# A routing chain rewritten with scans and one slot table, and TensorE products that nobody reads

## What is computed

```
h2 = x * (1 + sc2) + sh2
gl = h2 @ grp_w + grp_b                 # 4 groups
g_idx, pg_top = argmax(gl), softmax(gl)[g_idx]
sel = (h2 @ exp_w + exp_b).reshape(T, 4, 8)[g_idx]
vals, idx = top_k(sel, 2)               # 2 of the 8 experts of that group
w = pg_top * softmax(vals)
y += w_e * ((silu(h2 @ w_gate[e]) * (h2 @ w_up[e])) @ w_down[e])   # for the chosen e
```

## Time and profile before

| | |
|---|---|
| median of 3 runs | 1684.97 us (1683.86 to 1691.19) |
| profiled execution | 1687.71 us |
| its span, first to last instruction | 1684.5 us |
| mean granted TensorE clock | 0.938 of full |
| PE busy | 1506.4 us (89%) |
| DVE busy | 942.9 us (56%) |

### The profile page before, as it was taken

The page is one execution under the profiler, slowest core; times in us unless marked ns, Lnnn a source line. Parts: engine busy times, 40 slices in busy tenths (PEclk is TensorE's granted clock), DMA queues, the critical chain, the costliest instruction groups (busy, mean ns, idle before and its releaser), DMA issues. The chain is left out here.

```text
span 1684.5 us, 22742 instructions
## 1 busy us (share of the span) xinstructions
PE 1506.4 (89%) x8546; PEld 1091.8 (65%) x8546; DVE 942.9 (56%) x1580; ACT 370.5 (22%) x710; POOL 368.4 (22%) x624
## 2 busy tenths in 40 slices
PE   6689988999996999849999988998299999999985
PEld 2467766444444788638888874554288888888852
DVE  3867875466635999975665641534623333333326
ACT  2553342011110111135755550100000000000004
POOL 0330230111110000000312237654122122122204
PEclk9799999999998999979999988999579999999998
DMA  9422113233330221130000013113249898898845
GB/s 290 169 68 82 60 57 131 89 112 108 118 116 19 82 69 57 50 110 1 2 1 2 2 48 128 63 63 123 77 171 327 325 332 333 324 337 322 302 175 222
DMA packets 102965, 230.28 MB, mean 137 GB/s; under 512 B 12807, under 2 KB 70727, under 8 KB 94120
## 3 DMA queue, kind: packets, MB, share of 16 engines
q1 hardware_dynamic: 78968, 195.86, 32.8%
q0 software_dynamic: 10960, 20.80, 3.5%
q10 hardware_dynamic: 12960, 12.59, 2.2%
HBM read 204.66 MB, written 40.01 MB: 145 GB/s over the span
## 5 line engine op out<-in xcount | busy, mean ns | idle before, releaser
L1086 PE MATMUL PS<-buffer 128*128 128x128 f32 (+8 forms) x5674 | 1263.9, 381 | 107.5 <-DVE buffer L1576 52.0
L1086 PEld LDWEIGHTS PS<-buffer 128*128 128x128 f32 (+2 forms) x5674 | 879.7, 196 | 464.0 <-issue 309.0
L1576 DVE TENSOR_TENSOR buffer<-buffer 128x256 f32<-128x256 f32 (+18 forms) x467 | 264.8, 587 | 20.2 <-ACT buffer L836 5.6
L1089 PE MATMUL PS<-buffer 128*128 128x128 f32 x1176 | 166.7, 285 | 34.0 <-DVE buffer L1576 24.6
L1089 PEld LDWEIGHTS PS<-buffer 128*128 128x128 f32 x1176 | 137.9, 156 | 63.2 <-issue 49.1
L1576 DVE TENSOR_TENSOR buffer<-PS,buffer 128x512 f32<-128x512 f32 (+3 forms) x143 | 94.0, 684 | 144.2 <-PE PS L1086 126.2
L1576 DVE TENSOR_TENSOR buffer<-buffer,PS 128x256 f32<-128x256 f32 (+3 forms) x55 | 27.5, 501 | 206.4 <-PE PS L1086 195.8
L1996 DVE TENSOR_SCALAR_CACHE_REDUCE buffer<-PS 128x1152 f32<-128x1152 f32 (+1 forms) x72 | 89.2, 1239 | 41.5 <-PE PS L1086 40.5
L979 ACT ACTIVATE buffer<-buffer 128x1152 f32<-128x1152 f32 (+1 forms) x72 | 83.7, 1163 | 103.8 <-DVE buffer L1996 103.8
L1060 ACT ACTIVATE buffer<-PS 128x256 f32<-128x256 f32 x33 | 12.7, 384 | 371.3 <-PE PS L1086 293.3
L2012 DVE COPY buffer<-PS 128x640 f32<-128x640 f32 x64 | 52.8, 825 | 60.5 <-PE PS L1089 60.5
(11 more groups left out here) (162 smaller groups left out, 930.5 us busy)
## 6 DMA issues: line engine op xcount, KB each, us to landing
buffer<-in_exp_w_gate SPq DMA_DIRECT2D x33, 1024.0 KB
buffer<-in_exp_w_up SPq DMA_DIRECT2D x33, 1024.0 KB
buffer<-in_exp_w_down SPq DMA_DIRECT2D x33, 1024.0 KB
buffer<-in_w_mod SPq DMA_DIRECT2D x24, 1024.0 KB, 7.6
filter_spectra<-buffer ACTq DMA_DIRECT2D x88, 128.0 KB, 1.7
buffer<-filter_spectra SPq DMA_DIRECT2D x44, 256.0 KB, 2.6
buffer<-in_w_in SPq DMA_DIRECT2D x9, 1024.0 KB, 5.5
buffer<-expert_outputs SPq DMA_DIRECT2D x4, 1536.0 KB, 17.1
```

Of the source, the lines that this page charges most:

```text
L1086: return nc.tensor.matmul(out, lhsT, rhs, start=start, stop=stop)
L1089: return nc.tensor.transpose(out, in_, ident)
L1576: return dve.tensor_tensor(out, a, b, op)
```

## The change

1. Ahead of the routing chain: for the last tile DVE takes the logits of tile 6 before the moments rather than after `h2`; it makes `h2` from `resid` directly with two fused instructions, and `xnorm` behind it. POOL's last `x1` waits for `xnorm` (`xnorm_ready`).
2. Instructions that depend on no token move from the chain to a place before the first norm, with new tables (`overflow_base`, `tile_starts`, the token numbers in `slot_value`). The matrix `upper` becomes upper minus all-ones, since the table of running sums now includes the own tile.
3. The chain: the softmax exponents are shifted later and used later; the sum over tiles is one scan (`tensor_tensor_scan`) over data laid out expert by expert; the blocks come from a scaled and rounded count, their running sum from a scan; the block list is made last. Token number and weight lie side by side (`slot_value`), so one table `r_pair` 100 wide takes the place of `r_number` and `r_tok`, in two halves, one for each choice.
4. PE: 18 products for slots rather than 36, 9 of them after the first half; and `keep_clock`: 6, 8 and 4 products 256 columns wide of the identity with the tables, into bank 7, which nobody reads.
5. POOL gathers block 0 with `slot_token` as its index, without the copy.

The diff, cut where lines only move or rename:

```diff
@@ -213,7 +213,8 @@
-        mix_w = keep.take(2 * NTILE, "p (c t) -> p c t", c=2)
+        slot_value = keep.take(4 * NTILE, "p (c t s) -> p c t s", c=2, t=NTILE)
+        mix_w = slot_value[:, :, :, 1]
...
@@ -222,6 +223,8 @@
+        overflow_base = decay[:, 304:304 + NEXP]
+        tile_starts = mod_ring.rearrange("p r n -> p (r n)")[:, 0:NTILE * NEXP]
...
@@ -327,20 +330,21 @@
-        r_all = rt.take(NTILE * NEXP, "p (t n) -> p t n", t=NTILE)
-        r_before = rt.take((NTILE + 1) * NEXP, "p (t n) -> p t n", t=NTILE + 1)
-        r_count = rt.take(NEXP)
+        r_all = rt.take(NTILE * NEXP)
+        r_upto = rt.take(NTILE * NEXP)
...
-        r_scan = rt.take(2 * NEXP, "p (r n) -> p r n", r=2)
+        r_ends = rt.take(NEXP)
...
+        r_pair = rt.take(4 * NTILE * MAX_BLOCKS, "p (i s n) -> p i s n", i=2 * NTILE, s=2)
...
@@ -708,7 +712,7 @@
-                    pool.wait_ge(sem("h2_ready"), NTILE)
+                    pool.wait_ge(sem("xnorm_ready"), NTILE)
...
@@ -751,7 +755,10 @@
-            gather_rows(1, slice(0, 1), 1)
+            pool.indirect_dma_start(
+                out=xg[:, 1, :], out_offset=None, in_=h2_d[:, :],
+                in_offset=bass.IndirectOffsetOnAxis(ap=slot_token[:, 0:1], axis=0),
+                bounds_check=last_token, oob_is_err=False).then_inc(sem("xg_loaded1"), 16)
...
@@ -1477,28 +1484,31 @@
+            def keep_clock(count):
+
+                for i in range(count):
+                    mm(bank(7, 2 * P), ident, tables[:, 0:2 * P])
+
+            keep_clock(6)
...
-            flat = "p t n -> p (t n)"
-            mm(bank(0, NTILE * NEXP), upper, r_all[:, :, :].rearrange(flat), True, False)
-            mm(bank(0, NTILE * NEXP), ones, r_before[:, 0:NTILE, :].rearrange(flat), False, True)
-            mm(bank(1, NEXP), ones, r_before[:, NTILE, :]).then_inc(sem("routing_product"), 1)
+            mm(bank(0, NTILE * NEXP), upper, r_all, True, False)
+            mm(bank(0, NTILE * NEXP), ones, r_upto, False, True)
+            mm(bank(1, NEXP), ones, r_upto.rearrange("p (n t) -> p n t", t=NTILE)[:, :, NTILE - 1]).then_inc(sem("routing_product"), 1)
...
-            pe.wait_ge(sem("routing_ready"), 2)
-            for i in range(2 * NTILE):
-                last = mm(bank(4, MAX_BLOCKS), r_hot[:, i, :], r_number[:, i, :], i == 0, i == 2 * NTILE - 1)
+            keep_clock(8)
+            for c in range(2):
+                pe.wait_ge(sem("routing_ready"), 2 + c)
+                for i in range(NTILE * c, NTILE * (c + 1)):
+                    last = mm(bank(4, 2 * MAX_BLOCKS), r_hot[:, i, :], r_pair[:, i, :, :].rearrange("p s n -> p (s n)"),
+                              i == 0, i == 2 * NTILE - 1)
...
-            pe.wait_ge(sem("route_done"), 1)
+            pe.wait_ge(sem("control_ready"), 1)
...
+            keep_clock(4)
...
@@ -2035,26 +2045,42 @@
+                if t == NLAT:
+                    take_logits(t - 2)
...
-                give(dve.tensor_scalar(xnorm, resid, bn[:, 12:13], bn[:, 14:15], ALU.subtract, ALU.mult), "xnorm_ready")
...
-                    own(tt(h2, xnorm, sc2[1], ALU.mult))
-                    tt(h2, h2, sh2[1], ALU.add).then_inc(sem("h2_ready"), 1)
+                    own(dve.scalar_tensor_tensor(h2, resid, bn[:, 12:13], sc2[1], ALU.subtract, ALU.mult))
+                    dve.scalar_tensor_tensor(h2, h2, bn[:, 14:15], sh2[1], ALU.mult, ALU.add).then_inc(sem("h2_ready"), 1)
...
+                give(dve.tensor_scalar(xnorm, resid, bn[:, 12:13], bn[:, 14:15], ALU.subtract, ALU.mult), "xnorm_ready")
...
+            own(dve.tensor_scalar(overflow_base, first_slot, -1.0, float(P * (NEXP - 1)), ALU.mult, ALU.add))
...
+            own(dve.tensor_copy(slot_value[:, :, :, 0], token_no[:, 0:2 * NTILE].rearrange("p (c t) -> p c t", c=2)))
+            sub(upper, upper, ones)
+            for r in range(2):
+                dve.wait_ge(sem(f"mod_stored{r}"), 16 * ((MOD_CHUNKS - COND_CHUNKS) // 2))
+            own(dve.memset(tile_starts, 1.0))
+            own(dve.memset(tile_starts.rearrange("p (n t) -> p n t", t=NTILE)[:, :, 0], 0.0))
...
-                if t >= 3:
+                if t >= 3 and t != NTILE:
...
@@ -2073,101 +2099,80 @@
-            give(tt(r_g, groups, r_max.unsqueeze(2).broadcast_to([P, NTILE, NGRP]), ALU.subtract), "exponents_shifted")
-            dve.wait_ge(sem("exponents_taken"), 1)
-            own(dve.tensor_reduce(r_pg, r_exp, AX.X, ALU.add))
-            own(dve.reciprocal(r_pg, r_pg))
...
+            four = [P, NTILE, NGRP, EPG]
...
-            give(tt(r_d, r_v[:, 1, :], r_v[:, 0, :], ALU.subtract), "exponents_shifted")
-            dve.wait_ge(sem("exponents_taken"), 2)
...
-            own(tt(r_all, r_mask[:, 0, :, :], r_mask[:, 1, :, :], ALU.add))
-            own(dve.memset(r_before[:, 0, :], 0.0))
-            for t in range(NTILE):
-                ins = tt(r_before[:, t + 1, :], r_before[:, t, :], r_all[:, t, :], ALU.add)
-                own(ins) if t + 1 < NTILE else give(ins, "routing_ready")
...
+            own(tt(r_all.rearrange("p (n t) -> p t n", t=NTILE), r_mask[:, 0, :, :], r_mask[:, 1, :, :], ALU.add))
+            give(dve.tensor_tensor_scan(r_upto, tile_starts, r_all, 0.0, ALU.mult, ALU.add), "routing_ready")
+
+            give(tt(r_exp, groups, r_max.unsqueeze(2).broadcast_to([P, NTILE, NGRP]), ALU.subtract), "exponents_shifted")
+            give(tt(r_d, r_v[:, 1, :], r_v[:, 0, :], ALU.subtract), "exponents_shifted")
+
...
-            own(dve.tensor_copy(r_count, bank(1, NEXP)))
-            own(dve.tensor_scalar(r_blocks, r_count, float(P), None, ALU.is_gt))
-            for m in range(2, NTILE):
-                own(dve.scalar_tensor_tensor(r_blocks, r_count, float(P * m), r_blocks, ALU.is_gt, ALU.add))
...
+            count = bank(1, NEXP)
+            own(dve.tensor_scalar(r_blocks, count, 1.0 / P, -(0.5 + 0.5 / P), ALU.mult, ALU.add))
+            own(dve.tensor_scalar(r_blocks, r_blocks, ROUND_MAGIC, None, ALU.add))
+            own(dve.tensor_scalar(r_blocks, r_blocks, -ROUND_MAGIC, 0.0, ALU.add, ALU.max))
+            own(dve.tensor_tensor_scan(r_ends, ones[:, 0:NEXP], r_blocks, 0.0, ALU.mult, ALU.add))
+            sub(r_base, r_ends, r_blocks)
+            axpy(r_base, r_base, float(P), overflow_base)
+            rank = bank(0, NTILE * NEXP).rearrange("p (n t) -> p t n", t=NTILE)
...
-            for c in range(2):
-                own(tt(r_mask[:, c, :, :], r_mask[:, c, :, :], r_slot, ALU.mult))
-                own(dve.tensor_reduce(r_pos[:, NTILE * c:NTILE * (c + 1)], r_mask[:, c, :, :], AX.X, ALU.add))
+            own(tt(r_slots, r_mask, r_slot.unsqueeze(1).broadcast_to([P, 2, NTILE, NEXP]), ALU.mult))
+            own(dve.tensor_reduce(r_pos, r_slots.rearrange("p c t n -> p (c t) n"), AX.X, ALU.add))
...
-            give(tt(r_number, r_tok, token_no[:, 0:n].unsqueeze(2).broadcast_to(blocks_last), ALU.mult), "routing_ready")
-            give(tt(r_tok, r_tok, mix_w.rearrange("p c t -> p (c t)").unsqueeze(2).broadcast_to(blocks_last), ALU.mult), "routing_ready")
+            dve.wait_ge(sem("exponents_taken"), 2)
+            own(dve.tensor_reduce(r_pg, r_exp, AX.X, ALU.add))
+            own(dve.reciprocal(r_pg, r_pg))
+            own(dve.tensor_scalar(r_max, r_d, 1.0, None, ALU.add))
+            own(dve.reciprocal(r_max, r_max))
+            own(tt(mix_w[:, 0, :], r_pg, r_max, ALU.mult))
+            own(tt(mix_w[:, 1, :], mix_w[:, 0, :], r_d, ALU.mult))
+            for c in range(2):
+                i0, i1 = NTILE * c, NTILE * (c + 1)
+                own(tt(r_hot[:, i0:i1, :], row128.unsqueeze(1).broadcast_to([P, NTILE, P]),
+                       r_rowblk[:, 0, i0:i1].unsqueeze(2).broadcast_to([P, NTILE, P]), ALU.is_equal))
+                own(tt(r_blk[:, i0:i1, :], row128[:, 0:MAX_BLOCKS].unsqueeze(1).broadcast_to([P, NTILE, MAX_BLOCKS]),
+                       r_rowblk[:, 1, i0:i1].unsqueeze(2).broadcast_to([P, NTILE, MAX_BLOCKS]), ALU.is_equal))
+                both = [P, NTILE, 2, MAX_BLOCKS]
+                give(tt(r_pair[:, i0:i1, :, :], r_blk[:, i0:i1, :].unsqueeze(2).broadcast_to(both),
+                        slot_value[:, c, :, :].unsqueeze(3).broadcast_to(both), ALU.mult), "routing_ready")
+
+            blocks_first = [P, MORE_BLOCKS, NEXP]
+            own(tt(r_cmp, r_ends.unsqueeze(1).broadcast_to(blocks_first),
+                   row128[:, 0:MORE_BLOCKS].unsqueeze(2).broadcast_to(blocks_first), ALU.is_le))
+            own(dve.tensor_reduce(r_eid[:, 0:MORE_BLOCKS], r_cmp, AX.X, ALU.add))
+            own(dve.tensor_scalar(control[:, NEXP:MAX_BLOCKS], r_eid[0:1, 0:MORE_BLOCKS], float(NEXP - 1), None, ALU.min))
+            own(dve.tensor_scalar(control[:, 61:62], r_ends[0:1, NEXP - 1:NEXP], float(NEXP), None, ALU.add))
+            give(dve.tensor_scalar(control[:, 60:61], control[:, 61:62], 1, None, ALU.logical_shift_right), "control_ready")
...
-            own(dve.tensor_scalar(token, number, T + 0.5, -float(T), ALU.is_gt, ALU.mult))
```

(48 more changed lines are left out.)

25 lines of the change are left out of this document (5 added, 20 removed).

## The result

The changed kernel takes 1675.24 us (median of 5, 1672.6 to 1678.96) against 1683.93 (5, 1683.81 to 1691.19) for the kernel before in the same rounds. The ratio on record is 0.9921 with an interval of 0.9901 to 0.9941: 13.3 us, from 10 to 17. It is faster, by more than the 8.4 us that can be told from no change; the median lies in the range of 1660 to 1677 and 4.9 us above the 1670.3 forecast. The plain times lie closer together than the ratio says, by 8.7 us in their medians and 10.4 in their means, so the 13.3 is not to be read to a tenth of a us. A second measurement gave a ratio of 0.9914, with 12.6 us between the medians.

The account below looks back on a forecast made before the run. Expert blocks were taken as bound by PE, the stretch before them by DVE's chain. Terms 4.3 + 3.8 + 0 + 7.4 + 0.5 - 1.3 = 14.7 us took the median from 1684.97 to 1670.3 us; range 1660 to 1677.

Parts of the forecast that it names:

- ahead of the chain: Last tile before routing: early logits and `h2` ahead of `xnorm` start the chain 4.3 us earlier, at most 5.6.
- selection: DVE's routing, 11.37 us before: two exponents and nine additions go, a scan comes in; gain 3.8 us, 2.8 to 4.1.
- counting product: PE's product for the counts, 2.57 us at half clock: gain 0, up to 1.3 us at full clock.
- slots and tables: From the counts through tables and slot products, 25.0 us before: gain 7.4 us, 7.0 to 10.0.
- POOL's gather without the copy: From slots on PE to POOL's gather, 2.26 us before: dropping the copy gains 0.5 us, 0 to 0.8.
- the gather's collision: Block 0's gather now runs beside 3 MB of block 1's weights: 1.3 us lost, between 0 and 4.9.
- filler and block 0: Unread products in PE's gaps cost and gain nothing; up to 3.7 us in the first block at full clock.
- What bounds it: Expert blocks bound by PE, the stretch before by DVE's chain; each us saved there moves 33 blocks and tail forward whole.
- Moved instructions: Some twelve small instructions and two fills, about 3 us, lie in DVE's idle 18.29 us before its first norm: cost nothing.
- rival B: The gather's collision sets the first block: gather lands 4.9 us late, time 1673.9 us; chance 0.12.
- Rival A: The unread products hold PE's clock at full: gains of 19 to 25.5 us, time 1659.5 to 1666; chance 0.15.
- Rivals C and D: C: filler outlasts PE's gaps, 1685 to 1687 us, chance 0.08. D: expert loop becomes bound by transfers, 1693 us, chance 0.04.

Follow-up runs that it names:

- norm only: Kernel before with part 1 of the change alone (early logits, `h2` fused from `resid`, `xnorm` and `x1` behind): 1683.20 us, ratio 0.9966 to the kernel before.
- clock held: Changed kernel with more unread products, 7 ahead of the last transposes and 18, 18, 20 for 6, 8, 4: 1672.82 us, ratio 0.9895 to the kernel before.
- Late load: Changed kernel in which SP waits for block 0's rows before loading block 1's weights: 1673.16 us, ratio 0.9895 to the kernel before.
- late both: Changed kernel in which block 1's weights and ACT's `ln2` loads both wait for block 0's rows: 1669.65 us, ratio 0.9873 to the kernel before.
- no filler: Changed kernel without its 18 products that nobody reads: 1676.96 us, ratio 0.9913 to the kernel before.
- held, late load: Changed kernel with block 1's weights waiting for block 0's rows and unread products of 7, 18, 18, 16: 1663.82 us, ratio 0.9844 to the kernel before.

## Why the prediction was right, point by point

Terms by the profiled executions, each the length before less the length after, in us:

| term | forecast | measured |
|---|---|---|
| ahead of the chain | 4.3 (to 5.6) | 20.34 - 16.13 = 4.2 |
| selection | 3.8 (2.8 to 4.1) | 11.37 - 7.77 = 3.6 |
| counting product | 0 (to 1.3) | 0 |
| slots and tables | 7.4 (7.0 to 10.0) | 25.02 - 17.39 = 7.6 |
| POOL's gather without the copy | 0.5 (0 to 0.8) | 2.16 - 1.04 = 1.1 |
| the gather's collision | -1.3 (-4.9 to 0) | 7.15 - 10.89 = -3.7 |
| filler and block 0 | 0 (to 3.7) | 11.09 - 10.63 = 0.5 |
| sum | 14.7 | 13.3 |

The sum came out 1.4 us off with some luck: the collision alone took 2.4 more than its term, and POOL's copy and a shorter block 0 gave 1.1 back. The 0.5 of block 0 is chance rather than filler: its gate and up products took 9.97 and 9.61 us in the two profiles of before, 9.51 after, and 9.42 without the filler.

**What bounds it.** That the gap is bound by DVE's chain and passes through whole was right: from PE's turn to block 1 to the first read-back it is 379.40 us before and 379.41 after.

**Ahead of the chain** was right, and stands alone in norm only, to the same 4.21 us. The bound that was to end the gain at 5.6, POOL's `x1`, is real: with the clock held it is what the chain waits for. There it let through 5.3.

**Moved instructions** cost nothing, as forecast, thanks to the idle time around them. Their own size was put too low: DVE's idle time ahead of the first norm fell from 18.29 to 11.06 us, 7.2 rather than 3. Beside POOL's passes single ones took far more than the 0.19 assumed, as these rows of the timelines of DVE and POOL have it:

```profile
1026.90 2.40 DVE L2068 TENSOR_SCALAR buffer<-buffer 128x50 f32<-128x50 f32 x1
```

```profile
1026.91 2.34 POOL L700 TENSOR_TENSOR buffer<-buffer 128x1024 f32<-128x1024 f32 x1
```

The cover was wide enough for an estimate that was too low.

**Selection.** The scan was priced at the 576 row, 0.78, and took 0.77; the strided addition costs 0.68 against 0.47, the 0.2 allowed for.

**Slots and tables** came out within 0.2. The products 100 wide cost what those 50 wide did, and the first half was ready 9.8 us behind the counts against 9.6.

**POOL's copy** was mis-sized: I took half of the 1.1 us that copy and following issue fill, and all of it went. The upper bound of 0.8 was too low.

**The collision** is the term of the sum that was mis-sized most, by 2.4 us, 3.7 rather than 1.3: the steps were right (load sent 16.8 us behind the counts, as forecast; block 1's weights still in time), but the price was taken from the slowest of the later gathers, 8.4 us. The first gather has more beside it: the clearing scatters, the two `ln2` loads and 3 MB of weights, all at once. Late load and late both show it by taking them away, 10.9, 7.2, 4.4. "The gather lands 10 us or more after issue" was named as what would make the prediction wrong; it happened, and cost 2.4 us of the sum. The Trainium skill ("DMA: Bandwidth & Descriptors", section "SWDGE vs HWDGE vs iDMA") has the DMA engines take their queues in turn, from which 2.5 us were estimated; the trace goes with it in direction and lies further out, at 3.7. The median of 1675.24 is near rival B's 1673.9 and outside the forecast's own 1666 to 1674, but B's price of 4.9 was not reached, and the ratio, 13.3 us, lies in the forecast's own gain of 11 to 19.

**The filler** was costed at nothing, and no filler shows it. The reason given, idle time behind each set, is shown by clock held: with the idle filled the clock stays. Rival A was wrong of this kernel and right of the mechanism. One thing I did not foresee: the first two sets do raise the clock, to 1.00 for 3.4 and 6.8 us, only too early. "TensorE: Matmul & The Clock Gate" of the Trainium skill (section "What's actually happening") says that activity releases the throttle; the trace agrees, and adds that here it was given back before anybody used it.

Rivals C and D did not come about: 9.22 us of PE for slots and filler end ahead of the rows by 10.3, and the loop is not longer.

## What to carry to other kernels

Cost a serial chain instruction by instruction from the rows of the nearest shapes, and read the outcome from a mark just ahead of the change, not from the whole span: here the terms of DVE's chain came out within 0.2 us, while stages that nobody touched moved by 5. Price a transfer by what flows beside it at that moment, not by its fellows in the steady loop; moving a block list later also moves the loads that wait for it. Products that keep the clock up must reach the next real work; here, where they stopped 3.7 us or more short of it, they cost nothing and gave nothing.

## What the runs showed of the hardware that was not expected

- The same gather of 128 rows of 4 KB landed in 4.4 to 4.5 us with only the clearing scatters beside it, in 7.1 to 7.2 with the two `ln2` loads beside it and the weights either 10.8 us or more ahead or behind it, and in 10.5 to 11.2 with 3 MB of weights as well, sent 1.6 us ahead of it or, in clock held, 0.4 us behind.
- After 12 unread records 256 wide the granted clock stood at full for 3.4 us in which PE was busy 0.96; the same 2.08 us of idle time kept it in one execution and lost it in another. In held, late load it also fell while PE was busy, in the 36-wide products (2.06 us of 2.10, 1174.9 to 1177.0, behind 1.10 us of idle), and stayed at 0.50 through 4.00 us of busy time behind them.
- A running sum over 288 elements took 0.76 us, over 32 elements 0.22, where elementwise instructions of these sizes took 0.46 and 0.19; a 288-element addition that writes with a stride took 0.68. So each further element cost the running sum 2.1 ns and the others 1.0.
- A DVE instruction of 50 elements took 2.40 us (0.19 elsewhere), beginning and ending with a POOL pass of 2.34 us over 1024.
